# The first five levels of a delta rule's inverse as 32x32 blocks on the diagonal of the PE array, in a two-block mixer kernel

## The reference, cut to what matters

```python
diff = gcum[..., :, None] - gcum[..., None, :]
decay = jnp.exp(jnp.where(tri_incl, diff, -jnp.inf))
a_mat = jnp.where(tri_strict, jnp.einsum('nbhid,nbhjd->nbhij', kb, kc) * decay, 0.0)
t_mat = lax.linalg.triangular_solve(eye + a_mat, jnp.broadcast_to(eye, a_mat.shape),
                                    left_side=True, lower=True, unit_diagonal=True)
u = jnp.einsum('nbhij,nbhjd->nbhid', t_mat, vb)
w = jnp.einsum('nbhij,nbhjd->nbhid', t_mat, kb * jnp.exp(gcum)[..., None])
```

## Time and profile before

| | us |
|---|---|
| median of 3 runs | 1694.24 (1692.28 to 1694.34) |
| the profiled execution's own time | 1694.11 |
| its span | 1692.0 |
| TensorE busy in the span | 1572.8 |
| stage 0, steps 0 to 27 | about 218 to 280 us from the span's start |
| stage 1, steps 0 to 27 | about 318 to 380 us from the span's start |

### The profile page before, as it was taken

The page is one execution under the profiler, slowest core; times in us unless marked ns, Lnnn a source line. Parts: engine busy times, 40 slices in busy tenths (PEclk is TensorE's granted clock), DMA queues, the critical chain, the costliest instruction groups (busy, mean ns, idle before and its releaser), DMA issues.

```text
span 1692.0 us, 30969 instructions
## 1 busy us (share of the span) xinstructions
PE 1572.8 (93%) x11422; PEld 1380.7 (82%) x11422; DVE 1141.4 (67%) x1913; ACT 786.4 (46%) x1416; POOL 115.2 (7%) x130
## 2 busy tenths in 40 slices
PE   5899978789999999999989999999999889999998
PEld 3687768688777777788778589999898668999997
DVE  5975755554499999967455558885566665477644
ACT  2554543132354444432255457775444445566532
POOL 2000032220200000001000010001000001010000
PEclk8999988899999999999989999999899999999999
DMA  8344420000245555555432034556444223255562
GB/s 355 120 177 156 150 70 2 1 3 1 100 148 178 187 182 187 185 177 170 137 134 88 25 100 162 184 187 212 161 163 147 89 75 99 101 184 186 178 194 90
DMA packets 62906, 230.50 MB, mean 136 GB/s; under 512 B 6816, under 2 KB 8096, under 8 KB 62304
## 3 DMA queue, kind: packets, MB, share of 16 engines
q1 hardware_dynamic: 61408, 223.37, 38.8%
q0 software_dynamic: 1120, 5.54, 1.0%
q10 hardware_dynamic: 288, 0.33, 0.1%
HBM read 228.17 MB, written 1.05 MB: 135 GB/s over the span
## 4 chain that ended last, share of the span: by engine, by line
PE 79%; DVE 11%; ACT 5%; issue 3%; POOL 1%; DMA 1%; DVEq 0%; ACTq 0%; POOLq 0%
PE proj L646 21%; PE proj L648 20%; PE proj L647 20%; DVE w_low L2068 2%; PE bank L698 1%; ACT w_high L1571 1%; PE bank L901 1%; PE bank L918 1%; PE bank L1198 1%; PE bank L921 1%; DVE conv_mid L2148 1%; DMA ident_sb<-ident 1%; PE bank L949 1%; PE proj L1102 1%; DVE mod_products L2199 1%
## 5 line engine op out<-in xcount | busy, mean ns | idle before, releaser
L646 PE MATMUL proj<-h_high,w_high 128*128 128x256 f32 (+1 forms) x1768 | 583.7, 330 | 22.7 <-DVE h_low L2101 14.3
L648 PE MATMUL proj<-h_high,w_low 128*128 128x256 f32 (+1 forms) x1768 | 570.4, 323 | 0.0
L647 PE MATMUL proj<-h_low,w_high 128*128 128x256 f32 (+1 forms) x1768 | 570.1, 322 | 0.0
L2068 DVE TENSOR_TENSOR w_low<-w_raw,w_high 128x1024 fp32r<-128x1024 f32 x322 | 393.1, 1224 | 190.1 <-ACT w_high L1571 188.7
L1571 ACT ACTIVATE w_high<-w_raw 128x1024 fp32r<-128x1024 f32 x322 | 338.2, 1054 | 244.0 <-PE proj L648 240.4
L646 PEld LDWEIGHTS proj<-h_high,w_high 128*128 128x128 f32 x1768 | 335.9, 190 | 65.5 <-issue 18.5
L648 PEld LDWEIGHTS proj<-h_high,w_low 128*128 128x128 f32 x1768 | 336.4, 190 | 27.5
L647 PEld LDWEIGHTS proj<-h_low,w_high 128*128 128x128 f32 x1768 | 335.9, 190 | 25.0
L646 PE MATMUL proj<-act_high,w_high 128*128 128x256 f32 (+1 forms) x608 | 190.4, 313 | 0.4 <-DVE w_low L2068 0.4
L648 PE MATMUL proj<-act_high,w_low 128*128 128x256 f32 (+1 forms) x608 | 189.6, 312 | 0.0
L647 PE MATMUL proj<-act_low,w_high 128*128 128x256 f32 (+1 forms) x608 | 188.9, 311 | 0.0
(11 more groups left out here) (406 smaller groups left out, 1920.5 us busy)
## 6 DMA issues: line engine op xcount, KB each, us to landing
w_raw<-w_stream SPq DMA_DIRECT2D x322, 512.0 KB, 3.3
a_ring<-a_stream SPq DMA_DIRECT2D x80, 512.0 KB, 3.2
a_first<-a_head SPq DMA_DIRECT2D x4, 1024.0 KB, 17.9
a_first<-a_stream SPq DMA_DIRECT2D x4, 1024.0 KB, 18.6
x<-x_in SPq DMA_DIRECT2D x1, 2048.0 KB, 10.5
late_tab<-late_tables POOLq DMA_DIRECT2D x1, 1408.0 KB, 6.6
cond_rows<-cond_rows SPq DMA_DIRECT2D x1, 1024.0 KB, 5.9
cond_rows<-cond_rows POOLq DMA_DIRECT2D x1, 1024.0 KB, 5.1
```

Source lines behind the costliest of these rows:

```text
L646: mm(out_, wh, xh, start=first, stop=False)
L647: mm(out_, wh, xl, start=False, stop=False)
L648: return mm(out_, wl, xh, start=False, stop=last)
L2068: v.tensor_tensor(wl(n), RAW[:, n % 4, :], wh(n), ALU.subtract).then_inc(w_low, 1)
```

## The change

Levels 0 to 4 now keep blocks of at most 32x32 in a compact form, `TQ`: four blocks on the diagonal, 128 partitions by 32 columns for each head, the inverse and its transpose side by side. A product is four 32x32x32 matmuls, one for each quarter of the partitions (`QUARTERS`). So a first product of levels 1 to 4 is 16 matmuls in place of 8, and a second product of levels 1 to 3 is 32 in place of 16. At level 0 two products are formed (the negative and its transpose) with 32 matmuls in place of 8; `first_u` is gone. VectorE updates inverse and transpose of levels 0 to 3 with one operation of 128x256 in place of two.

At level 4 (`QLEV - 1`) the second product has 64 matmuls: each 32x32 tile is a product and, added in PSUM, the identity times the old block. VectorE then writes all of `TU` with one operation of 128x512 (block times an indicator of the quarter, which also makes the zeros; the memset is gone), and ScalarE writes `TT` with two operations of 128x128, one step later, after the copy of the next step (`lv_t4`). Levels 5 and 6 are as before, except that they read the halves out of `TU`.

```diff
+        QUARTERS = [slice(32 * i, 32 * i + 32) for i in range(4)]
+        IN_HALF = [slice(32 * (i % 2), 32 * (i % 2) + 32) for i in range(4)]
+        QLEV = 5
...
# TensorE, first product
+                    elif lev < QLEV:
+                        pe.wait_ge(G["lv_tu"], at + (k - 1 if k < 6 else k - 3))
+                        out_ = heads_of(b, 32)
+                        for h in range(HEADS):
+                            for x, y in zip(QUARTERS, IN_HALF):
+                                last = mm(out_[x, h, :], CT[x, b, h, y], TQ[x, q, 0, h, :], start=True, stop=True)
...
+                        if lev == QLEV:
+                            pe.wait_ge(G["lv_t4"], 4 * st + q + 1)
...
# TensorE, second product
+                    if lev < QLEV - 1:
+                        both = pair_of(2 + 2 * b)
+                        for h in range(HEADS):
+                            for x in QUARTERS:
+                                mm(both[x, 0, h, :], TQ[x, q, 1, h, :], M1[x, b, h, 0:32], start=True, stop=True)
+                        for h in range(HEADS):
+                            for x in QUARTERS:
+                                last = mm(both[x, 1, h, :], M1[x, b, h, 0:32], TQ[x, q, 1, h, :], start=True, stop=True)
...
+                    if lev == QLEV - 1:
+                        for h in range(HEADS):
+                            for x in QUARTERS:
+                                mm(out_t[x, h, :], TQ[x, q, 1, h, :], M1[x, b, h, 0:32], start=True, stop=False)
+                            for x in QUARTERS:
+                                mm(out_t[x, h, :], TQ[x, q, 1, h, :], ID[x, x], start=False, stop=True)
...
# GpSimd
-                        if 2 <= k < 6:
-                            pool.wait_ge(G["lv_u"], 4 * st + k - 1)
...
-                        nc.gpsimd.memset(TU[:], 0.0).then_inc(G["u_zero"], 1)
...
# ScalarE
+                    if LEVELS[k - 1][0] == QLEV - 1:
+                        act.wait_ge(G["lv_x"], (NSTEP - 4) * st + k - 4)
+                        for c in range(2):
+                            last = f(TT[:, LEVELS[k - 1][1], :, 32 * c:32 * c + 32], heads_of(2 + 2 * ((k - 1) % 2), 32), ACT.Copy, scale=gtab("half", c, 1))
+                        last.then_inc(G["lv_t4"], 1)
...
# VectorE
-                            v.tensor_tensor(TT[:, q, :, :], TT[:, q, :, :], halves_of(2 + 2 * b), ALU.subtract)
-                        if lev < NLEV - 2:
-                            last = v.tensor_tensor(TH[:, q, :, :], TH[:, q, :, :], new, ALU.subtract)
+                        if lev < QLEV - 1:
+                            last = v.tensor_tensor(TQ[:, q, :, :, :], TQ[:, q, :, :, :], pair_of(2 + 2 * b), ALU.subtract)
+                        elif lev < QLEV:
+                            last = v.tensor_tensor(TU[:, q, :, :].rearrange("p h (c j) -> p h c j", c=4),
+                                                   heads_of(3 + 2 * b, 32).unsqueeze(2).to_broadcast([P, HEADS, 4, 32]), quarter, ALU.mult)
```

More of the change, by code:

```diff
@@ L49 @@
 NCOLS = _n
-GDN_TABLES = [("cum", 2 * P), ("neg", 2 * P), ("eye", 64), ("lev", 12 * 64)]
+GDN_TABLES = [("cum", 2 * P), ("neg", 2 * P), ("eye32", 32), ("half", 2), ("quarter", 4), ("lev", 12 * 64)]
 LATE_TABLES = [("perm64", P), ("perm32", P), ("cm", SEQ), ("sm", SEQ), ("c64", SEQ), ("s64", SEQ), ("c32", SEQ),
@@ L381, in two_blocks_kernel @@
         TT = place("inv_t", [P, 4, HEADS, 64])
-        TH = place("inv_u_halves", [P, 4, HEADS, 64])
+        TQ = place("inv_quarters", [P, 4, 2, HEADS, 32])
         TU = place("inv_u", [P, 4, HEADS, P])
@@ L913, in second_product @@
                         pe.wait_ge(G["lv_tu"], at + k - 1)
-                    out_t, out_u = (BK[i + 2 * b][:, 0:4 * 64].rearrange("p (h j) -> p h j", h=HEADS) for i in (2, 3))
+                    if LEVELS[k - 2][0] == QLEV - 1:
+                        pe.wait_ge(G["lv_t4"], 4 * st + LEVELS[k - 2][1] + 1)
+                    if lev < QLEV - 1:
[6 more added lines that the diff above has]
+                                last = mm(both[x, 1, h, :], M1[x, b, h, 0:32], TQ[x, q, 1, h, :], start=True, stop=True)
+                        last.then_inc(G["lv_x"], 1)
+                        return
+                    if lev == QLEV - 1:
+                        out_t, out_u = heads_of(2 + 2 * b, 32), heads_of(3 + 2 * b, 32)
+                        for h in range(HEADS):
+                            for x in QUARTERS:
+                                mm(out_t[x, h, :], TQ[x, q, 1, h, :], M1[x, b, h, 0:32], start=True, stop=False)
+                            for x in QUARTERS:
+                                mm(out_t[x, h, :], TQ[x, q, 1, h, :], ID[x, x], start=False, stop=True)
+                        for h in range(HEADS):
+                            for x in QUARTERS:
+                                mm(out_u[x, h, :], M1[x, b, h, 0:32], TQ[x, q, 1, h, :], start=True, stop=False)
+                            for x in QUARTERS:
+                                last = mm(out_u[x, h, :], ID[x, x], TQ[x, q, 1, h, :], start=False, stop=True)
+                        last.then_inc(G["lv_x"], 1)
+                        return
+                    out_t, out_u = heads_of(2 + 2 * b, 64), heads_of(3 + 2 * b, 64)
                     if lev < NLEV - 1:
@@ L2330, in _ @@
             for st in range(2):
[L2331 to L2338, removed]
+                eye = gtab("eye32", 0, 32).unsqueeze(1).to_broadcast([P, 2 * HEADS, 32])
+                quarter = gtab("quarter", 0, 4).unsqueeze(1).unsqueeze(3).to_broadcast([P, HEADS, 4, 32])
                 if st:
@@ L2345, in _ @@
                         triangles(1, q + 1)
[L2346 to L2352, removed]
                 for k, (lev, q) in enumerate(LEVELS):
```

46 lines of the change are left out of this document (27 added, 19 removed).

## The result

The changed kernel takes 1735.89 us (median of 4 runs, 1731.02 to 1739.82) against 1694.29 us for the kernel before in the same session: a ratio of 1.0247, 95% interval 1.0220 to 1.0274. It is 41.6 us slower, where 12.5 us faster was forecast. The profiled execution took 1731.02 us, with a span of 1729.1.

What follows compares the result with a forecast made beforehand. Dense parts were taken as bound by TensorE's first and second products, elsewhere by VectorE, ScalarE or other work. Stage 0's 6.5 us and stage 1's 8.0 make 14.5, less 2.0 for the clock: 12.5 off 1694.11 gives 1681.6, range 1675 to 1696.

Steps and rivals of the forecast that it cites:

- A quad's time: Products of levels 0 to 4: four small tiles at once take 31.5 ns, 7.9 ns a row; dense steps 0.75 to 0.85 us.
- The rival that rows can't start so close: All compact levels: 29.2 ns a row is the queue's own rate, so doubled rows cost double; 1744 us, chance 0.09.
- term (a): Start of stage 0: the wait for `first_u` goes and step 2's product waits for the first update; saves 0.8 us.
- the transposes of step 6: Stage 0, a sign that the forecast is right: these transposes start near 231.9 us.
- the first rival: Dense steps and level 4: instruction packets, 1.2 us each, hold up TensorE; up to 5.8 us, 1687; mild form chance 0.15.
- the rival's last sentence: Both stages: if each packet started only after the last was used up, the gain would be gone altogether; chance 0.04.
- The clock, priced at 2.0 us: Both stages: TensorE idles more between shorter bursts, so one or two low-clock stretches on dense steps take 2.0 us off.
- The rival that it stays low: Both stages: four small tiles fill a quarter of the array and the clock stays at 1.2 GHz; 1705 us, chance 0.06.
- terms (b) to (f): Later steps: stage 0 saves 0.9, 2.0, 1.5, 1.3, 0 us; stage 1 saves 2.9, 1.4, 1.1, 1.6, nothing.

Runs made afterwards that it cites:

- burst_straight: Kernel before with 576 more products of 32x32x32 written out at the end of TensorE's program: 1718.57 us against 1692.58 (one run).
- loop_st1_b: Changed kernel with steps 5 to 16 of stage 1 as a three-turn TensorE loop, one-row one-column dummy products, spatial products behind it: 1748.13 us (one run).
- pair_wide: Kernel before with inverse and transpose side by side, both made by products at level 0, still in 64x64 halves: 1691.03 us against 1693.91, ratio 0.9982.
- loop_st1: Changed kernel with steps 5 to 16 of stage 1 as a three-turn TensorE loop, other work moved ahead of or behind it: 1747.38 us, ratio 1.0330.
- burst_loop: Kernel before with 576 more products of 32x32x32 at its end, as a loop of six turns: 1702.84 us against 1692.58 (one run).
- burst64_straight: Kernel before with 576 more products of 64x64x64 in two halves written out at its end: 1719.47 us.

## Why the prediction was wrong, point by point

**A quad's time: right.** At full clock the 32 rows of a first product start over 0.26 us (forecast 0.25), the 64 of a second over 0.55 to 0.58 (0.50), and where both were at hand a step began 0.90 us after the last (353.93 to 354.83; forecast 0.75 to 0.85). Against the 0.47 of the earlier trace rows the small tiles did what they were to do. The rival that rows can't start so close is out: across four tiles they came 8.3 to 8.8 ns apart.

**The start of stage 0, term (a): right in kind.** The wait for `first_u` is gone, and the second pair's products began at 221.43 against 223.40. The gain was lost at once, in a pause of 2.61 us at 224.06, and the transposes of step 6 began at 234.32, not at 231.9 (before 233.51).

**The step that failed: the first rival, "the instructions don't arrive fast enough".** Its reckoning of the need was right (0.75 packets a step, 1.25 at level 4; the 83 packets measured agree). Its price was not: "a packet takes 1.2 us ... 0.91 us if they follow one another without a pause". 1.2 us is how long a packet is on its way (0.9 to 1.5 measured), not how often one can come. They came every 3.75 us in the burst, and no two closer than 3.3 in any of the kernels run, so a dense step costs 0.75 x 3.75 = 2.8 us and a step of level 4 4.7, against 1.40 before. The rival's price of 5.8 us should have been of the order of 24 x 1.4 + 8 x 3.3 = 60 us less what other work covers; 33 us of pauses were found. The sentence "nothing in the trace asks for more than a quarter of that rate" was the sign that was misread, and it doesn't hold: dense steps of before use 128 rows in 3.73 us, a third of one packet per 1.2 us. The earlier trace rows give nine packets for 62 us, but they don't come evenly. Had the packets' starts been set beside the dense steps, two of them 4.17 us apart (251.62 and 255.79) would have been seen on each side of such steps. A supply that has never been seen faster than the need is not shown to be faster. And the rival's last sentence, with a chance of 0.04, ended at "the gain would be gone altogether", where the doubled count of instructions makes a loss of it. Whether a packet really starts only after the last is used up stays open.

**The clock, priced at 2.0 us: wrong in size, and its share of the loss is open.** The traces show the clock as a share of full speed alone: what the prediction calls 1.2 and 2.4 GHz is 0.50 and 1.00 there. The low clock covers 20.5 us from 219.2 and 30.7 us from 256.8 in stage 0 alone. Where packets set the pace here it cost nothing (a packet every 3.75 us in `burst_straight` at 0.50, 4.0 and 3.6 apart in the changed kernel at 1.00). Elsewhere it lengthens TensorE's work, as the 2.00 us of the spatial products show, and the steps of the loop in `loop_st1_b` took 1.82 us at it. The forecast that idle between bursts brings it was right in the bursts. The rival that it stays low has part of the truth: it was low for 107 of the 159 us of the two stages. How the loss splits between pauses and clock stays open, since TensorE's 25 us more on the chain, of which the low clock's part was not measured, stand against 22 less of the other engines.

**VectorE and ScalarE, terms (b) to (f).** The pauses hide whether they were right. `pair_wide` is the nearest test of the terms that don't need small tiles (the start, one update for two), and it gave 3 us.

## What to carry to other kernels

Count instructions as well as their time. For code written out, a dense stretch of TensorE needed 29 ns a matmul row with its weight load here (128 rows in 3.75 us), so smaller tiles that doubled the rows lost where the large ones (29.2 ns a row) took no more than that already. Loops of up to 800 instructions were exempt (77 packets in `loop_st1` against 83, 65 in `burst_loop` against 73). Compare the need with the closest spacing of packets that the trace shows, not with the duration of one. And other work placed among dense steps isn't idle ballast: moving it out cost 20 us here, in part because it had filled pauses.

## What was not expected of the hardware

- Instruction packets of TensorE's straight code came 3.5 to 4.4 us apart (3.75 from pause to pause in a steady stretch) with hardly another transfer under way (DMA share 0.02), though each was on its way for 0.9 to 1.4 us. The closest two in all these traces are 3.3 us apart. Why they don't overlap is not shown.
- A loop of 384 instructions (`burst_loop`) and one of about 800 (the stages) fetched nothing after their first turn: no packet on q8 after 1689.35 in the one, none between 351.81 and 370.36 in `loop_st1_b`.
- Four 32x32 tiles on the diagonal took a row every 8.3 to 8.8 ns at a granted clock of 1.00 and every 13.3 at 0.50 (32 rows in 0.43 us, `loop_st1_b`); two 64x64 tiles one every 29.2 at 1.00 (`burst64_straight`).
- The granted clock stayed at 0.50 for 41 us of `loop_st1_b` in which TensorE was busy for 35.2, while in `burst_loop` it went back to 1.00 after 3.4 us (1688.5 to 1691.9). In `loop_st1` it was 0.50 from 339.0 to 354.9, a stretch of 128-wide products in which TensorE was never idle. What decides it was not tried.
